# First feed-forward matmul: 14 low halves made by ScalarE and an adding DMA in place of VectorE

## What is computed

```python
def second_block(x, ...):
    ...
        h = layer_norm(DEEPNORM_ALPHA * h + m @ w_out[l], ln1_g[l], ln1_b[l])
        f = jnp.square(jax.nn.relu(h @ w_ff1[l])) @ w_ff2[l]
        h = layer_norm(DEEPNORM_ALPHA * h + f, ln2_g[l], ln2_b[l])
```

## Time and profile before

| What | us |
|---|---|
| Median of 3 runs | 1141.18 |
| Lowest and highest | 1139.32, 1141.46 |
| Span of the profiled execution | 1139.6 |
| TensorE busy in it | 1114.3 |
| VectorE busy | 601.2 |
| ScalarE busy | 419.0 |
| GpSimd busy | 85.9 |

### The profile page before, as it was taken

One profiled execution on the slowest core, in us unless ns is written; L12 is line 12 of the kernel. 1 busy time (PEld: TensorE's weight loads), 2 busy tenths in 40 slices (PEclk: granted clock), 3 DMA queues, 4 the chain that ended last, 5 costly groups with the idle time before them and its releaser, 6 DMA issues.

```text
span 1139.6 us, 13000 instructions
## 1 busy us (share of the span) xinstructions
PE 1114.3 (98%) x5404; PEld 934.6 (82%) x5404; DVE 601.2 (53%) x668; ACT 419.0 (37%) x446; POOL 85.9 (8%) x95
## 2 busy tenths in 40 slices
PE   8999999999999999999699999999999999999996
PEld 8788888887888888888588888888888888888885
DVE  5553357546544565558465654766332334435446
ACT  7444442543343422343333633332232223332330
POOL 3000000000022000006200000121000000000002
PEclk8999999999999999999799999999999999999999
DMA  8523421223324422231222222361423323323221
GB/s 280 180 77 111 147 75 40 82 74 111 111 75 159 126 104 74 80 124 38 74 74 74 77 72 74 108 224 59 126 78 106 109 75 111 98 86 111 78 70 74
DMA packets 82737, 114.79 MB, mean 101 GB/s; under 512 B 4316, under 2 KB 57948, under 8 KB 82560
## 3 DMA queue, kind: packets, MB, share of 16 engines
q1 hardware_dynamic: 79648, 103.19, 27.7%
q0 software_dynamic: 2752, 10.76, 2.7%
q10 hardware_dynamic: 288, 0.13, 0.0%
HBM read 109.87 MB, written 4.20 MB: 100 GB/s over the span
## 4 chain that ended last, share of the span: by engine, by line
PE 89%; DVE 5%; POOL 2%; issue 2%; ACT 1%; DMA 0%; DVEq 0%; POOLq 0%; SPq 0%; ACTq 0%
PE bank L369 27%; PE bank L371 27%; PE bank L370 27%; PE bank L477 2%; PE bank L671 1%; DVE w_lo L1162 1%; POOL rstd_tmp L1781 1%; DVE residual L1599 1%; PE bank L597 1%; PE bank L578 1%; DVE bn L1466 1%; PE bank L727 1%; PE bank L630 1%; PE bank L615 1%; DVE v_hat L1473 1%
## 5 line engine op out<-in xcount | busy, mean ns | idle before, releaser
L1162 DVE TENSOR_TENSOR w_lo<-w_raw,w_hi 128x2048 fp32r<-128x2048 f32 (+1 forms) x92 | 209.7, 2281 | 281.3 <-ACT w_hi L871 279.1
L369 PE MATMUL bank<-act_t_hi,w_hi 128*128 128x512 f32 (+1 forms) x832 | 321.4, 386 | 11.2 <-ACT u_gelu L1048 10.7
L371 PE MATMUL bank<-act_t_hi,w_lo 128*128 128x512 f32 (+1 forms) x832 | 318.2, 382 | 0.0
L370 PE MATMUL bank<-act_t_lo,w_hi 128*128 128x512 f32 (+1 forms) x832 | 317.9, 382 | 0.0
L871 ACT ACTIVATE w_hi<-w_raw 128x2048 fp32r<-128x2048 f32 (+1 forms) x91 | 172.0, 1892 | 204.1 <-PE bank L371 191.6
L369 PEld LDWEIGHTS bank<-act_t_hi,w_hi 128*128 128x128 f32 x832 | 157.2, 189 | 41.8 <-issue 11.7
L371 PEld LDWEIGHTS bank<-act_t_hi,w_lo 128*128 128x128 f32 x832 | 157.0, 189 | 30.5
L370 PEld LDWEIGHTS bank<-act_t_lo,w_hi 128*128 128x128 f32 x832 | 157.3, 189 | 29.9 <-issue 0.2
L369 PE MATMUL bank<-w_hi,x_hi 128*128 128x512 f32 x416 | 162.2, 390 | 0.0
L371 PE MATMUL bank<-w_hi,x_lo 128*128 128x512 f32 x416 | 161.9, 389 | 0.0
L370 PE MATMUL bank<-w_lo,x_hi 128*128 128x512 f32 x416 | 161.8, 389 | 0.0
(11 more groups left out here) (262 smaller groups left out, 1077.6 us busy)
## 6 DMA issues: line engine op xcount, KB each, us to landing
w_raw<-in_w_in SPq DMA_DIRECT2D x46, 1024.0 KB, 5.1
w_raw<-in_w_ff SPq DMA_DIRECT2D x32, 1024.0 KB, 5.2
w_raw<-in_w_out SPq DMA_DIRECT2D x10, 1024.0 KB, 5.2
w_raw<-in_w_mem_kv SPq DMA_DIRECT2D x3, 1024.0 KB, 6.6
residual<-in_x SPq DMA_DIRECT2D x4, 512.0 KB, 9.6
x_spill<-residual POOLq DMA_DIRECT2D x1, 2048.0 KB, 7.1
residual<-x_spill POOLq DMA_DIRECT2D x1, 2048.0 KB, 9.7
out<-residual SPq DMA_DIRECT2D x3, 512.0 KB, 2.6
```

The lines of the kernel that those rows point to most:

```text
L369: pe.matmul(dst, lh, rh, start=start, stop=False)
L370: pe.matmul(dst, lh, rl, start=False, stop=False)
L371: return pe.matmul(dst, ll, rh, start=False, stop=stop)
L1162: return dve.tensor_tensor(dst, src, hi.bitcast(f32), ALU.subtract)
```

## The change

For blocks 2 to 15 of ff1 the low half is made differently. ScalarE, having written the high half to `WH`, writes the same rounded values negated to `WL`. GpSimd waits for that and issues a DMA that adds the raw block to `WL`: source `RAW`, destination `WL`, both in SBUF, 1 MB, with the addition done in the transfer. VectorE waits for the DMA's semaphore in place of subtracting, and counts `w_lo` up as before. TensorE waits both for `w_lo` and for the DMA's semaphore. SyncE still loads block n+2 when `w_lo` says that block n's low half is finished. The rstd steps of GpSimd are divided: four before the 14 DMAs, four behind them.

```diff
--- before.py
+++ after.py
@@ -256,6 +256,7 @@
         w0_loaded, w_half_hi = sem("w_block0_first_half_loaded"), sem("w_block1_2_first_half_hi")
         w0_hi, w0_lo = sem("w_block0_second_half_hi"), sem("w_block0_second_half_lo")
         own_lo = sem("w_lo_done_by_gpsimd")
+        w_minus_hi, lo_summed = sem("w_minus_hi_done"), [sem(f"w_lo_summed_by_dma{i}") for i in range(2)]
         x_hi, x_lo = sem("x_hi_done"), sem("x_lo_done")
         bank_full = [sem(f"bank_full{b}") for b in range(8)]
         bank_free = [sem(f"bank_free{b}") for b in range(8)]
@@ -794,6 +795,7 @@
                     n = ff1_0 + 2 + b
                     wh, wlo = weights(n, (WH, WL))
                     pe.wait_ge(w_lo, i * 2 + (n + 1))
+                    pe.wait_ge(lo_summed[b], i * 16 + 16)
                     for t in range(2):
                         pe.wait_ge(bank_free[t], i * 2 + (u0[t] + b))
                         for k in range(KC):
@@ -1110,12 +1112,17 @@
                     q = (2 * m + t) % 4 * S
                     act.activation(F1[:, group, q:q + S], bank[t][:, :], ACT.Relu).then_inc(bank_free[t], 1)
 
+            def split_minus(n, loads, more):
+
+                split(n, loads, more)
+                act.activation(WL[n % 2][:, :], RAW[n % 2][:, :], ACT.Copy, scale=-1.0).then_inc(w_minus_hi, 1)
+
             split(ff1_0 + 1)
             relus(0, 0)
             with act.Fori(0, 7) as i:
-                split(ff1_0 + 2, i * 16, i * 2)
+                split_minus(ff1_0 + 2, i * 16, i * 2)
                 relus(1, i, i * 2)
-                split(ff1_0 + 3, i * 16, i * 2)
+                split_minus(ff1_0 + 3, i * 16, i * 2)
                 relus(2, i + 1, i * 2)
             split(ff2_0)
             act.wait_ge(f1_done, 4)
@@ -1730,9 +1737,11 @@
             split(ff1_0 + 1)
             squares(0, 0)
             with dve.Fori(0, 7) as i:
-                split(ff1_0 + 2, i * 2)
+                dve.wait_ge(lo_summed[0], i * 16 + 16)
+                dve.sem_inc(w_lo, 1)
                 squares(1, i, i * 2)
-                split(ff1_0 + 3, i * 2)
+                dve.wait_ge(lo_summed[1], i * 16 + 16)
+                dve.sem_inc(w_lo, 1)
                 squares(2, i + 1, i * 2)
             split(ff2_0)
             split_x(0, E_FF2, F1[:, 0, :])
@@ -1852,9 +1861,18 @@
             load_all(L2G[:, :], a["ln2_g_2"][0], ln2_in)
             load_all(L2B[:, :], a["ln2_b_2"][0], ln2_in)
             split_own(ff1_0)
-            for j in range(2 * TT):
+
+            def row_rstd(j):
                 pool.wait_ge(ln_var, TT + j + 1)
                 rstd(RST[:, j % TT:j % TT + 1], MV[:, j % TT, 1:2], 1, 1.0, LN_EPS)
+
+            for j in range(TT):
+                row_rstd(j)
+            for m in range(14):
+                pool.wait_ge(w_minus_hi, m + 1)
+                pool.dma_start(WL[m % 2][:, :].bitcast(f32), RAW[m % 2][:, :], accum_op=ALU.add).then_inc(lo_summed[m % 2], 16)
+            for j in range(TT, 2 * TT):
+                row_rstd(j)
 
 
         @block.sync
```

## The result

The changed kernel takes 1154.03 us (median of 4 runs, 1153.30 to 1154.91) beside 1140.36 us for the kernel before on the same chip (4 runs, 1139.32 to 1141.46). The ratio is 1.0122, with a 95% interval of 1.0109 to 1.0135. The time lost is 13.7 us; the sum of the prediction was 13.6.

A forecast was written before the change was run, and what follows sets the result against it. TensorE bounds the kernel, so the change can only cost: 6.8 us in the steady loop, 4.0 at its first block and 2.8 of clock make 13.6; 1141.2 + 13.6 = 1154.8 us, 1.2% slower, range 1143 to 1190.

The forecast's parts named there:

- TensorE bounds, and there is nothing to win: In ff1 TensorE goes from matmul to matmul without idle time, hiding VectorE's subtraction; the change can only cost.
- The threshold of D, 5.97 us: In ff1's steady loop, D is the sum's time from issue to landing; above 5.97 us TensorE waits.
- D = 7.1 us: The 1 MB sum takes 7.1 us from issue to landing, like a 2 MB spill out of SBUF.
- Every second block of the steady loop pays e = 1.13 us, 6.8 in all: In ff1's loop, every second block starts e = D - 5.97 late, about 1.1 us each, 6.8 us in sum.
- The first block, 4.0 us: At the loop's first block (block 2), raw data arrives later, so TensorE stalls 4.0 us; block 3 is covered.
- The clock, 2.8 us once: After the 4.0 us stall TensorE's clock falls to 1.2 GHz, costing 2.8 us once; stalls of 1.1 us cost nothing.
- B: Rival: the sum is as quick as a copy; only the loop's first block pays, 2.1 us, time 1143.3; chance 0.17.
- C: Rival: adding limits or sum meets raw load, D 8 us and more; 49 us lost at D 9.7, 1190; chance 0.28.

The follow-up runs named there:

- experiment 2: Kernel before plus ScalarE's second pass alone, writing the negated high half; VectorE subtracts as before, but after it: 1139.99 us, ratio 0.9992.
- experiment 5: Changed kernel with the loop's first turn by VectorE's subtraction and the negated half written first in the 12 blocks after it: 1140.34 us, ratio 1.000.
- experiment 7: Changed kernel with a GpSimd memset of an unused tile before each of the 14 DMA issues, making them 1.84 us later: 1173.36 us, ratio 1.0286.
- experiment 1: Changed kernel with the addition left out of the 14 transfers, a plain copy within SBUF (result not the network's): 1142.04 us, ratio 1.001.
- experiment 4: Changed kernel with ScalarE's two passes exchanged, negated half first, high half made while the DMA runs: 1144.93 us, ratio 1.0035.
- experiment 8: Changed kernel with the low half divided: the DMA sums columns 0 to 1023, VectorE subtracts the rest beside it: 1141.39 us, ratio 1.0014.
- experiment 3: Changed kernel with the loop's first turn (blocks 2 and 3) made by VectorE's subtraction, blocks 4 to 15 by the DMA: 1148.44 us, ratio 1.0068.
- experiment 6: Changed kernel with 16 matmuls into an unused bank between block 1 and the ff1 loop, filling the first gap: 1152.75 us, ratio 1.0106.

## Why the prediction was right

Its steps, in its order.

*TensorE bounds, and there is nothing to win.* Right: experiments 2 and 5, in which no block is late, are both level with the kernel before, though VectorE is rid of 12 subtractions in 5 and of none in 2.

*The threshold of D, 5.97 us.* Its terms, measured at block 4 from the end of block 2 at 820.73: high half begins 0.78 us later (0.79 taken), the two passes take 3.71 (3.72), from there to GpSimd's issue 0.29 (0.1 taken, from a subtraction of GpSimd behind a wait; experiment 7 shows 0.30 before the issue too, behind GpSimd's own memset), the sum 6.96 (7.1), landing to TensorE 0.29 with VectorE's relay in it (0.3 and 0). Together 12.03 where 12.01 was put down. Two errors of 0.1 to 0.2 us cancelled. Experiments 1, 4 and 8 lie below the threshold, each by another term (D 4.5; 1.8 us less ahead of the issue; D 4.6), and in all three the stalls of the steady loop are gone.

*D = 7.1 us.* Measured 7.0. It was chosen by the row it was thought nearest to, 2 MB out of SBUF, for the reason that a sum reads 2 MB to write 1. Experiment 1 backs the reason and doesn't prove it: without the addition the same transfer takes half the engines' time, but no row shows the second read. That the size came out so near owes something to luck: the spill crosses to HBM, and the sum doesn't.
*Every second block of the steady loop pays e = 1.13 us, 6.8 in all.* The place and number are right; the size is 1.28, 7.7 in all, because a stall of 1.15 us is followed by a second matmul 0.1 us late, a term that the prediction lacked. Experiment 3 showed this part alone: 7.3 us. That every second block pays is not a law, as experiment 6 shows: there odd blocks waited too for a while, with the same total, and the prediction would have read that as a collision in each of them, where one slow sum at the start was enough.

*The first block, 4.0 us.* Measured 4.2, and the 0.2 is the issue of GpSimd again (0.30 from the negated half's end at 799.29).

*The clock, 2.8 us once.* Measured 2.8, from 806.1 to 812.9, and taken away by experiment 6. The stalls of 1.15 us left the clock alone, as said. That the clock would fall was well founded; that it cost just 2.8 us is in part luck. The prediction took the size from one execution's return after a gap of 10.7 us. Behind the same gap in the ten profiles here the clock came back 2.8 to 5.9 us after work resumed, so at half speed 1.4 to 2.9 us were lost, and the stall of 6.1 us in experiment 7 cost 2.0.

*The rivals.* B, as quick as a copy: the adding is not free, 7.0 against 4.5 us; experiment 1 is what B would have been, and its time, 1142.0, is near the 1143.3 put down for it. C, the collision: it was to raise all of the sums and doesn't, since 13 of 14 land in 6.9 to 7.0 us. But something like it exists: the sum of block 3 goes out 0.67 us behind the raw load of block 4 and takes 10.5, and the load takes 6.5 instead of 5.2. The rows show no other large transfer beside the two; no run takes the load away, so the cause is argued. The prediction had tied this to a large e; what brings it about is the late first block, whose landing releases the raw load just when ScalarE has the next operand ready. It cost nothing here, as the slow block 2 ran long enough. C's price, that every stall of some 3.7 us loses the clock for 2.8 us, looks too high by experiment 7, though its stalls are a little shorter: two of six that cost 3.2 us lost nothing more, and four lost 1.6.

## What to carry to other kernels

Where a bound engine takes blocks from two buffers, compare the length of the whole preparation, from the buffer's release to the engine's start, with the length of a block: below it a slower way of making the operand is free, above it the lateness is paid once for every two blocks, however the two share it. Put the step with the longest transfer behind it first on the preparing engine, and look at the loop's first turn by itself, where the buffers' history differs: here these two orders of work made the difference between 13.7 us and nothing. Moving work off VectorE, which was not the bound, brought no time: experiment 5 freed 27.5 us of it and took as long as before.

## What the runs showed of the hardware

An accumulating DMA within SBUF takes nearly twice the engines' time of a copy of the same size, 5.1 against 2.7 us for 1 MB, and 7.0 against 4.5 us to landing. A sum issued 0.7 us behind a 1 MB load from HBM took 10.5 us (10.5, 11.1 and 10.7 at the same place in experiments 6, 4 and 7).

After a short gap the clock is not a matter of the gap's length alone. Idle times of TensorE of 1.0 and 1.4 us left it at 1.00; one of 2.2 us (experiment 4) and four of six of 2.9 us (experiment 7) were followed by the lower level, which began 0.7 to 1.5 us after work had resumed and cost 1.6 us; those of 4.0 and 5.9 us had it fall before work resumed, and cost 2.8 and 2.0. (These idle times are the bracketed figures of the rows.) What tells the two of 2.9 us that lost nothing from the four that did, these runs don't show.

The clock is low for a time at two places ahead of ff1 in all ten profiles, and for how long differs between executions of the same code. The first is the startup. TensorE has a gap there ahead of a group of small transposes, 1.97 us before 8.07 in the kernel before, 2.62 us before 7.95 in the changed one. In the changed kernel's execution the clock was at its lower level from the slice of 7 to 8 us until 10.8:

```profile
7.00:8.00 1.00, 0.05 (x1) 0.08 (x2) 0.75 (x1) 0.59 (x3) 0.44 (x2) 0.68 1.09 352
...
10.00:11.00 1.00, 1.00 (x8) 1.00 (x6) 0.40 (x1) 0.58 (x2) 0.00 (x0) 0.61 1.10 347
```

and in that of the kernel before from 9 us until the slice of 15 to 16 us (granted clock 0.60 in it, 0.50 in the one of 14 to 15). The second is the gap of 10.72 us, which has the same length in every profile. The clock returned 5.6 us after work had resumed in the kernel before, but 3.0 us after in experiment 3:

```profile
551.51 0.77 PE L370 MATMUL bank<-act_t_hi,w_hi 128*128 128x512 f32 x1 [10.72 <-ACT u_gelu L1056]
```

```profile
554.00:555.00 1.00, 1.00 (x4) 0.82 (x4) 1.00 (x1) 0.00 (x0) 0.00 (x0) 0.74 0.00 0
```

From that matmul to the first of ff1 are 234.4 us in the kernel before and 233.2 us in experiment 3. The end of the 10.72 us gap itself moves by 1.6 us between the profiles, the stretch behind it by 1.4 us, and the start of ff1 by 3.0 us (784.70 to 787.66); the edits all change work that runs later. A difference of up to 3 us between two single profiles of this kernel can therefore not be put down to an edit unless its place is found in the rows.
